# A second operator on GpSimd's multiplications by a column of c

## The reference, cut to what matters

```python
c_act = jax.nn.silu(c)
mod = c_act @ w_ada[l] + b_ada[l]                  # 2048 x 12288; the second block has its own, 2048 x 6144
sh1, sc1, gt1, sh2, sc2, gt2 = jnp.split(mod[:, None, :], N_MOD, axis=-1)
h = _rmsnorm(x, norm1_g[l]) * (1.0 + sc1) + sh1
p = h @ w_in[l]                                    # then a recurrent mixer and a pooling mixer
x = x + gt1 * mix
h = _rmsnorm(x, norm2_g[l]) * (1.0 + sc2) + sh2
x = x + gt2 * _conv_ffn(h, w_up[l], conv_w[l], conv_b[l], w_down[l])
# second block: projections, two attention branches, and an output product
x = x + gate[:, None, :] * rms_norm(out, g_post[layer])
```

## Time and profile before

| | us |
|---|---|
| median of 3 runs | 2772.86 |
| lowest and highest run | 2759.91, 2775.61 |
| span of the profiled execution, from the first to the last instruction | 2768.1 |

### The profile page before, as it was taken

One profiled execution on the slowest core, in us unless ns is written; L12 is line 12 of the kernel. 1 busy time (PEld: TensorE's weight loads), 2 busy tenths in 40 slices (PEclk: granted clock), 3 DMA queues, 4 the chain that ended last, 5 costly groups with the idle time before them and its releaser, 6 DMA issues.

```text
span 2768.1 us, 47948 instructions
## 1 busy us (share of the span) xinstructions
PE 2643.3 (95%) x20992; PEld 2397.8 (87%) x20992; DVE 1864.0 (67%) x2268; ACT 1082.6 (39%) x1255; POOL 1128.9 (41%) x612
## 2 busy tenths in 40 slices
PE   5689989999999999999999999999999999999997
PEld 2268877778999999999999899989988898999996
DVE  1248863267988888888887775576446874786454
ACT  1133422144434444343446443444334444444353
POOL 0293011013899999999991475862000000000001
PEclk7689989899999999999999999999999999999998
DMA  8967647676877777777765776775767665666664
GB/s 314 321 180 187 183 153 256 221 230 191 228 218 240 240 240 240 240 243 244 243 221 138 190 194 201 209 209 171 183 193 187 161 174 179 172 168 168 183 185 120
DMA packets 759185, 568.49 MB, mean 205 GB/s; under 512 B 46497, under 2 KB 645665, under 8 KB 758849
## 3 DMA queue, kind: packets, MB, share of 16 engines
q1 hardware_dynamic: 758976, 565.42, 69.7%
HBM read 563.29 MB, written 2.10 MB: 204 GB/s over the span
## 4 chain that ended last, share of the span: by engine, by line
PE 80%; DMA 6%; POOL 6%; DVE 5%; ACT 1%; issue 1%; SPq 1%; DVEq 0%; POOLq 0%
PE bank L785 15%; PE bank L768 9%; PE bank L769 9%; PE bank L772 9%; PE bank L788 8%; PE bank L752 5%; PE bank L754 5%; PE bank L753 5%; PE bank L1009 2%; DMA ada<-w_ada 2%; PE bank L741 2%; PE bank L821 2%; PE bank L822 2%; PE bank L823 2%; POOL prod_e L625 1%; POOL prod L625 1%
## 5 line engine op out<-in xcount | busy, mean ns | idle before, releaser
L1737 DVE TENSOR_TENSOR w_low<-ring,w_high 128x2048 fp32r<-128x2048 f32 x388 | 951.2, 2452 | 341.9 <-ACT w_high L1337 334.8
L1337 ACT ACTIVATE w_high<-ring 128x2048 fp32r<-128x2048 f32 x388 | 738.5, 1904 | 368.7 <-DMA ring<-w_in 127.6
L768 PE MATMUL bank<-acts,w_high 128*128 128x256 f32 x2400 | 586.4, 285 | 0.0
L769 PE MATMUL bank<-acts,w_high 128*128 128x256 f32 x2400 | 583.6, 283 | 0.0
L785 PE MATMUL bank<-acts,w_high 128*128 128x512 f32 (+1 forms) x2064 | 502.3, 396 | 11.1 <-DVE acts L1804 6.4
L768 PEld LDWEIGHTS bank<-acts,w_high 128*128 128x128 f32 x2400 | 461.6, 192 | 1.1 <-issue 0.2
L769 PEld LDWEIGHTS bank<-acts,w_high 128*128 128x128 f32 x2400 | 461.7, 192 | 0.0
L785 PEld LDWEIGHTS bank<-acts,w_high 128*128 128x128 f32 (+1 forms) x2064 | 382.7, 190 | 89.9 <-DVE acts L1804 6.5
L625 POOL TENSOR_SCALAR prod<-adf,cact 128x512 f32<-128x512 f32 x165 | 378.8, 2296 | 22.2 <-DMA adf<-w_ada 6.1
L639 POOL TENSOR_TENSOR sumf<-sqf 128x256 f32<-128x256 f32 x1 | 0.7, 743 | 789.7 <-ACT sqf L1718 789.7
L772 PE MATMUL bank<-acts,w_low 128*128 128x256 f32 x2400 | 312.4, 283 | 0.0
(11 more groups left out here) (457 smaller groups left out, 3711.2 us busy)
## 6 DMA issues: line engine op xcount, KB each, us to landing
ring<-w_in SPq DMA_DIRECT2D x182, 1024.0 KB, 5.8
ring<-w_up SPq DMA_DIRECT2D x88, 1024.0 KB, 5.9
ada<-w_ada SPq DMA_DIRECT2D x76, 1024.0 KB, 6.2
adf<-w_ada SPq DMA_DIRECT2D x44, 1024.0 KB, 8.1
ring<-w_down SPq DMA_DIRECT2D x44, 1024.0 KB, 6.4
ring<-w_out SPq DMA_DIRECT2D x16, 1024.0 KB, 6.0
adg<-w_ada SPq DMA_DIRECT2D x64, 256.0 KB, 5.6
ring<-w_mla SPq DMA_DIRECT2D x16, 1024.0 KB, 5.5
```

The costliest lines, as they stand in the source:

```text
L768: pe.matmul(o, wh[:, j], AH[:, j, :], start=j == 0, stop=False, skip_group_check=True)
L769: pe.matmul(o, wh[:, j], AL[:, j, :], start=False, stop=False, skip_group_check=True)
L1337: act.activation(WH[s][:, 0:WIDE[n]], ring[s][:, 0:WIDE[n]], ACT.Copy).then_inc(high_done, 1)
L1737: v.tensor_tensor(WL[s][:, 0:WIDE[n]], ring[s][:, 0:WIDE[n]], f32(WH[s][:, 0:WIDE[n]]), ALU.subtract)\
```

## The change

The multiplications of L623, L625 and L689 are one instruction each: a tensor and, as its operand, one number for each partition. Before, the instruction has one operator and its second is empty. After, the second operator is a multiplication by the constant 1.0, which stands in the instruction. The values are the same. No instruction is added, removed or moved on any engine; on GpSimd 272 instructions are encoded otherwise.

```diff
                         if q == j == 0:
-                            ins = pool.tensor_scalar(acc[:, :], w[:, j, :], col, None, ALU.mult)
+                            ins = pool.tensor_scalar(acc[:, :], w[:, j, :], col, 1.0, ALU.mult, ALU.mult)
                         else:
-                            after(pool.tensor_scalar(prod[:, :], w[:, j, :], col, None, ALU.mult))
+                            after(pool.tensor_scalar(prod[:, :], w[:, j, :], col, 1.0, ALU.mult, ALU.mult))
...
-                    pool.tensor_scalar(o, AG[k % 2][:, :].rearrange("p (a b) -> p a b", a=2), cact[:, DT + j:DT + j + 1], None,
-                                       ALU.mult).then_inc(g_free, 1)
+                    pool.tensor_scalar(o, AG[k % 2][:, :].rearrange("p (a b) -> p a b", a=2), cact[:, DT + j:DT + j + 1], 1.0,
+                                       ALU.mult, ALU.mult).then_inc(g_free, 1)
```

## The result

The changed kernel takes 2818.37 us (median, 2817.76 to 2821.99), the kernel before 2767.31 us in the same comparison: a ratio of 1.0194, 95% interval 1.0166 to 1.0222, about 51 us more. The forecast was no change.

What follows compares the result with a forecast made beforehand. PE was taken as the bound, POOL close behind in the feed-forward part. With unchanged durations the terms sum to 0; the median less 1 us for a possible small shortening gives 2772 us, range 2758 to 2785, 80% range 2750 to 2836.

Steps and rivals of the forecast that it cites:

- the stages: The early, feed-forward and attention stretches where GpSimd works, each checked for what PE does meanwhile.
- 1.9 + 1: Most that a shortening could gain: 1.9 us of PE waits early, and 1 us in attention.
- 8.6 us: Most that a shortening could gain in the feed-forward stretch, at its start: 5.9 us PE idle, 2.7 us clock.
- the chain's 6% of POOL: POOL's share, beside PE's 80%, of the chain that ended last; said to look like the price at stake but not be.
- d = 0: Change in duration of one 128x512 GpSimd multiplication, taken as none from 1.56 us; bounds -0.6 and +1.56 us.
- The lower bound of 0.95 us: Shortest duration allowed for a 512-column GpSimd multiplication, from L660's 1.896 us for 1024 columns.
- rival 1: GpSimd's multiplications get clearly shorter, about -0.6 us each, nearly all hidden by PE: 2761 us; chance of shorter 0.36.
- at most the loss at 780 to 810 us: Cap on a shortening's gain in the feed-forward stretch: PE's idle time and lowered clock at its start, 8.6 us.
- 11.5 us: All PE losses hanging on POOL: 1.9 early, 8.6 feed-forward, 1 attention; the most any shortening could gain.
- Rival 2: Multiplications get longer and POOL bounds the feed-forward part; SP's wait for a quarter holds up ring loads; chance of longer 0.32.
- mild form: Multiplications 0.30 us longer: 7 us early, 33 us feed-forward, attention 0, so 2813 us.
- full form: Multiplications 1.56 us longer: 37 us early, 255 us feed-forward, 10 us attention, so 3075 us.

Runs made afterwards that it cites:

- e2: Two operators only in the early and attention multiplications, the feed-forward turns keep one as in the kernel before: 2763.05 us, ratio 0.9982.
- e3: Changed kernel with GpSimd's feed-forward multiplications and additions replaced by memsets: 2744.9 us, ratio 0.9915 to the kernel before.
- e8: Changed kernel with ten small memsets on GpSimd after each feed-forward multiplication: 2831.12 us, ratio 1.0225 to the kernel before.
- e4: Changed kernel with five small memsets on GpSimd after each feed-forward multiplication: 2761.48 us, ratio 0.9984 to the kernel before.

## Why the prediction was wrong, point by point

- **Reading the stages was right in the main.** The early stretch hung on POOL by no more than a few us: the shorter multiplication gains 4.8 us outside the feed-forward part (e2, interval 1.7 to 8.0), where the prediction allowed 1.9 + 1. Too low was what hung on GpSimd inside that part: the prediction allowed 8.6 us, and without any arithmetic there (e3) the kernel is 18 us faster than e2. That the chain's 6% of POOL were not the price at stake is shown by the changed kernel, where POOL has gone from the chain and the time is longer.
- **The duration was wrong.** d = 0 was taken; it is -0.87 us, and outside the bounds too. The lower bound of 0.95 us came from the fastest elementwise row at hand (L660), which is another instruction and no bound for this one. The reason given in rival 1, that a one-tensor instruction slower than a two-tensor one is not set by its reading, was borne out.
- **The step that failed is the value of a shortening.** The prediction let a shorter multiplication gain "at most the loss at 780 to 810 us" and wrote 11.5 us "whatever d is". It named the missing term itself, that "the two engines shut each other out, so d is paid by both", but then summed POOL's turn and PE's idle time alone. DVE was not in the sum, though its rounds of 12.4 us had no room beside PE's 11.6. Where rival 1 does name DVE, it has the sign wrong: it expects DVE to be "shut out less often". With the free part of the old multiplication gone, DVE's L2164 met an addition 53 times in 85 instead of 5 in 88. The term missing is 74.9 - 69.6 = 5.3 us a turn, over 11 turns about 58 us; 56 were measured.
- **Rival 2 had the right side and the wrong cause.** The time lies between its mild form and its full form, but GpSimd did not become the bound; it idles a third of each turn. That mechanism exists (e8), at about two thirds of the price: 70 us over e4 where 107 were expected. So it is luck that the 80% range, 2750 to 2836 us, holds the measured time: its upper part was there for a longer multiplication.
- **What the prediction said would show it wrong did:** PE's time in the feed-forward part was to stay full if the instruction got shorter. It fell to 477.31 of 500 us.

## What to carry to other kernels

Before an engine off the critical path is made faster, look at which resource it shares with one that is nearly as busy as the bound: here GpSimd's additions shut out DVE's two-tensor instructions, and the later part of GpSimd's slow multiplication was the gap that DVE lived on. Read the neighbour's durations instruction by instruction in the stretch, not only its busy share, and compare its round with the bound's. Work in the background was better spread than done fast here: the same instruction at a slower pace gave all of the time back, and in shorter bursts three quarters of it.

## What the runs showed of the hardware that was not expected

- GpSimd's multiplication of 128x512 by a column takes 1.56 us with one operator and 0.69 us with two, the second a multiplication by 1.0.
- Both forms of the multiplication delay a two-tensor DVE instruction alike at their start: an L2164 that started within the first 0.11 us took 0.86 to 0.89 us, in the one-operator form and in the other. All 61 that started 0.87 us or later in the one-operator form took the undisturbed 0.48 to 0.49 us.
- Beside a GpSimd addition (1.26 us) L2164 took 1.47 us instead of 0.48; beside the two-operator multiplication L2165 took 0.80. Memsets on GpSimd at the same places left it at 0.485 us (e3).
- What in GpSimd's program makes the one-operator form longer, no run here shows.
